# A third plain tile at the head of each FFN layer, and VectorE splitting the weight sums of four items

## What is computed

```python
def conv_ffn(h, w_up, conv_w, conv_b, w_down):
    u = causal_dwconv(h @ w_up, conv_w) + conv_b          # w_up: 1024 x 5632, 3 taps
    gate, up = jnp.split(u, 2, axis=-1)                   # 2816 columns each
    return (jax.nn.silu(gate) * up) @ w_down              # w_down: 2816 x 1024

x = x + conv_ffn(rmsnorm(x, ffn_norm[layer]), ffn_w_up[layer], ffn_conv_w[layer], ffn_conv_b[layer], ffn_w_down[layer])
```

## Time and profile before

| | us |
|---|---|
| median of 3 runs | 2227.12 (2222.16 to 2233.1) |
| profiled execution | 2223.45 |
| its span, first to last instruction | 2221.7 |
| PE / DVE / ACT / POOL busy | 2072.0 / 1409.0 / 1102.0 / 1140.4 |
| matmuls of the items (line 1184) | 4704 in the trace, 380 to 383 ns each by their spans |

### The profile page before, as it was taken

The page is one execution under the profiler, slowest core; times in us unless marked ns, Lnnn a source line. Parts: engine busy times, 40 slices in busy tenths (PEclk is TensorE's granted clock), DMA queues, the critical chain, the costliest instruction groups (busy, mean ns, idle before and its releaser), DMA issues. The chain is left out here.

```text
span 2221.7 us, 30110 instructions
## 1 busy us (share of the span) xinstructions
PE 2072.0 (93%) x11310; PEld 1002.4 (45%) x11310; DVE 1409.0 (63%) x2247; ACT 1102.0 (50%) x1653; POOL 1140.4 (51%) x856
## 2 busy tenths in 40 slices
PE   6989967889799999999999999899989999998998
PEld 3544425654344444444444444455434444443444
DVE  8788888857776575574544032795867467466452
ACT  6459856634564564554323211643566456454420
POOL 6104424216776766757584032303776766766642
PEclk8999989999999999999999999899999999999999
DMA  4001100002021211111232011101111211211112
GB/s 171 20 10 48 34 27 1 13 19 73 29 60 55 67 57 57 58 48 57 68 110 58 0 30 33 44 2 53 53 38 48 68 57 54 69 57 48 58 36 97
DMA packets 186494, 110.20 MB, mean 50 GB/s; under 512 B 4351, under 2 KB 180902, under 8 KB 186358
## 3 DMA queue, kind: packets, MB, share of 16 engines
q1 hardware_dynamic: 185894, 107.00, 16.2%
q0 software_dynamic: 464, 1.39, 0.2%
HBM read 104.18 MB, written 4.19 MB: 49 GB/s over the span
## 5 line engine op out<-in xcount | busy, mean ns | idle before, releaser
L1184 PE MATMUL ps<-arena 128*128 128x512 f16 x2784 | 612.9, 380 | 21.6 <-DVE arena L2695 9.1
L1184 PEld LDWEIGHTS ps<-arena 128*128 128x128 f16 x2784 | 272.5, 98 | 356.0 <-issue 23.6
L1184 PE MATMUL ps<-h_hi,arena 128*128 128x512 f16 x1280 | 393.8, 383 | 15.1 <-POOL arena L839 9.3
L759 POOL TENSOR_SCALAR w_scaled<-stage 128x1024 f32<-128x1024 f32 (+4 forms) x82 | 79.4, 969 | 609.2 <-PE ps L1054 419.4
L1184 PE MATMUL ps<-h_lo,arena 128*128 128x512 f16 x640 | 245.1, 383 | 0.0
L2678 DVE SCALAR_TENSOR_TENSOR work<-ps,fvec,work 128x1023 f32<-128x1023 f32 (+1 forms) x176 | 221.4, 1279 | 17.9 <-ACT work L1893 14.8
L1184 PEld LDWEIGHTS ps<-h_hi,arena 128*128 128x128 f16 x1280 | 126.1, 99 | 171.0 <-issue 14.9
L1054 PE MATMUL ps<-h_hi,arena 128*128 128x512 f16 x704 | 183.0, 381 | 2.8 <-ACT small L1799 1.7
L1054 PE MATMUL ps<-arena 128*128 128x512 f16 x708 | 158.6, 386 | 13.5 <-DVE xT L2558 6.4
L813 POOL TENSOR_TENSOR w_scaled<-stage 128x512 f32<-128x512 f32 (+2 forms) x64 | 73.4, 1148 | 175.2 <-ACT stage L1632 174.9
L1632 ACT ACTIVATE stage<-stage 128x2048 f32<-128x2048 f32 (+2 forms) x62 | 104.6, 1687 | 110.4 <-DMA stage<-in_ffn_w_up_dram 93.3
(11 more groups left out here) (358 smaller groups left out, 3779.8 us busy)
## 6 DMA issues: line engine op xcount, KB each, us to landing
stage<-in_ffn_w_up_dram SPq DMA_DIRECT2D x84, 512.0 KB, 3.8
stage<-in_ffn_w_down_dram SPq DMA_DIRECT2D x48, 384.0 KB, 3.5
stage<-in_od_w_in_dram SPq DMA_DIRECT2D x20, 512.0 KB, 3.8
stage<-in_ev_w_in_dram SPq DMA_DIRECT2D x12, 512.0 KB, 3.7
arena<-in_x_dram SPq DMA_DIRECT2D x8, 512.0 KB, 7.0
stage<-in_ffn_w_down_dram SPq DMA_DIRECT2D x16, 256.0 KB, 2.7
out_dram<-arena SPq DMA_DIRECT2D x8, 512.0 KB, 3.0
stage<-in_od_w_out_dram SPq DMA_DIRECT2D x12, 256.0 KB, 2.8
```

The lines of the kernel that those rows point to most:

```text
L759: nc.gpsimd.tensor_scalar(scaled, src, W_SCALE, 1.0, ALU.mult, ALU.mult).then_inc(w_parts, 1)
L1184: last = mm(ps[:, bank, :], left, b[:, k, :], start=(fresh and k == 0 and pss == 0), stop=(k == nk - 1 and pss == 2), skip_group_check=True)
```

## The change

Four things are done, in both layers.

1. Tile 2 is made by plain products too, behind tile 1. The two are now called `FIRST` and `SECOND` (items -2 and -1). `ITEMS` begins at tile 3, and the bank set of an item is `(p + 1) % 2`. Tile 2's halves lie in the stage buffer, are scaled one by one, split in a high part by ACT and a low part by POOL, 1024 elements each, and have no sums.
2. The orders of ACT, DVE, POOL and SP at the head of the layer are rewritten around that.
3. `split_sums` on DVE takes the place of `su_low_sums` on POOL for the items with `LAST_DOWN - PAIRS + 1 < p <= LAST_DOWN + 1`: down items 1, 2 and 3 of the four-tile group and the up item behind them (tile 17).
4. The split hidden tiles are laid out by tile (`gated`), no longer by block. The data are the same.

Core of the diff:

```diff
-            ITEMS += [("up", f) for f in range(2 if _g == 0 else _f0 + 1, _f0 + _nf)]
+            ITEMS += [("up", f) for f in range(3 if _g == 0 else _f0 + 1, _f0 + _nf)]
...
+        def by_vector(p):
+            return LAST_DOWN - PAIRS + 1 < p <= LAST_DOWN + 1
...
SP, ffn_stream
+                sp.wait_ge(w_split, unit0[f"up{layer}"] + 2)
+                load_raw(SECOND, 0)
+                load_raw(SECOND, 1)
                 for p in range(NI):
-                    if p == 0:
-                        sp.wait_ge(w_split, unit0[f"up{layer}"] + 2)
...
+                    sp.wait_ge(su_read_up, up_read(layer, raw_before(p)))
...
POOL, ffn_split
                 first_low(layer, 1)
+                second_low(layer, 0)
+                second_low(layer, 1)
                 su_first(layer, 0)
                 su_second(layer, 0)
-                su_low_sums(layer, 0)
                 top_low(layer, 1, 1, 1)
                 top_low(layer, 2, 3, 2)
+                su_low_sums(layer, 0)
                 su_first(layer, 1)
                 top_low(layer, 3, 4, 3)
                 su_second(layer, 1)
...
-                    su_low_sums(layer, p)
+                    if not by_vector(p):
+                        su_low_sums(layer, p)
...
PE, ffn
+                def plain(p):
+                    q, s = su_of(layer, p), bank_set(tile_of(p))
...
+                    for g in range(2):
+                        if p == FIRST:
+                            pe.wait_ge(*((su_read, X0 + q + 1) if g else (gate_low, GATE_LOW0 + layer + 1)))
+                        elif g == 0:
+                            pe.wait_ge(hid_f, FT * layer + tile_of(p - 2) + 1)
+                            pe.wait_ge(su_read, X0 + q + 1)
+                        else:
+                            set_free(p - 2)
+                            pe.wait_ge(su_read_up, up_read(layer, p))
...
+                plain(FIRST)
+                plain(SECOND)
...
ACT, ffn
-                if p == 0:
-                    act.wait_ge(unit_done, ring0[f"up{layer}"])
-                elif p == 1:
-                    act.wait_ge(unit_done, ring0[f"plain{layer}"] + 2)
+                if p < 2:
+                    act.wait_ge(unit_done, ring0[f"plain{layer}"] + 2 * p + 2)
...
-                        if f == 1:
-                            act.wait_ge(t_low, X0 + 3 * layer + 3)
+                        if f in (1, 3):
+                            act.wait_ge(t_low, X0 + 3 * layer + f)
...
-                su_hi_raw(layer, 0)
                 tap2(0, 0)
                 tap2(0, 1)
-                su_hi_sums(layer, 0)
+                second_raw_high(layer, 0)
+                second_raw_high(layer, 1)
+                silu(0)
+                highs(0)
                 top_high(3, 1)
                 top_high(3, 0)
                 top_high(3, 2)
-                silu(0)
-                highs(0)
-                su_scale(layer, 1)
+                su_scale(layer, 0)
                 tap2(1, 0)
                 tap2(1, 1)
-                act.wait_ge(unit_done, ring0[f"plain{layer}"] + 2)
+                su_hi_raw(layer, 0)
+                su_hi_sums(layer, 0)
+                silu(1)
+                highs(1)
+                su_scale(layer, 1)
+                tap2(2, 0)
+                tap2(2, 1)
+                act.wait_ge(unit_done, ring0[f"plain{layer}"] + 4)
                 top_high(4, 3)
...
DVE, ffn
+                def split_sums(p):
+                    nk = tiles_of(p)
...
+                    dve.wait_ge(su_hi, hi_count(layer, p))
+                    dve.wait_ge(su_sum, X0 + 4 * cross_of(layer, p) + 4)
+                    dve.wait_ge(su_read, X0 + su_of(layer, p) + 1)
+                    V.tensor_tensor(lo[:, S1:S3 + 1, :], sums_a, hi[:, S1:S3 + 1, :], ALU.subtract)
+                    V.tensor_tensor(lo[:, S2:S4 + 1, :], sums_b(nk), hi[:, S2:S4 + 1, :], ALU.subtract).then_inc(su_split, 1)
...
+                top_sum(0)
                 conv(0)
+                top_sum(1)
+                chain_begin(0)
+                top_sum(2)
+                top_sum(3)
+                chain_end(0)
                 dve.wait_ge(t_hi, X0 + 4 * layer + 2)
                 V.tensor_tensor(top_lo[:, 0], n12, top_hi[:, 0], ALU.subtract).then_inc(t_made, 1)
-                chain_begin(0)
                 conv(1)
-                chain_end(0)
+                chain_begin(1)
+                chain_end(1)
+                conv(2)
                 for p in range(NI):
...
                     cross(p, U2)
-                    if p and before is not None:
+                    if before is not None:
                         chain_begin(before)
                     cross(p, U3)
                     cross(p, C22)
-                    if p == 0:
-                        chain_begin(before)
                     if before is not None:
                         chain_end(before)
+                    if by_vector(p + 1):
+                        split_sums(p + 1)
                     cross(p, C21)
```

More of the change, by code:

```diff
@@ L409, in bank_set, with bank_of @@
             return f % 2
+        def bank_of(p):
+            return (p + 1) % 2
         def su_of(layer, p):
-            return layer * (NI + 1) + p + 1
+            return layer * (NI + 2) + p + 2
         def cross_of(layer, p):
@@ L419, in hi_count @@
         def hi_count(layer, p):
-            return layer * (2 * NI + 1) + 2 * (p + 1) + 1
+            return layer * (2 * NI + 3) + 2 * (p + 2) + 1
         def t_at(layer, f, op):
@@ L488, in by_tile, with up_read @@
             return ap.rearrange("p s (i c) -> p s i c", c=P)
+        def up_read(layer, p):
+            return MASK_STEPS + layer * (NI + 1) + p + 2
         def raw_before(p):
@@ L1095, in ffn, with set_free @@
                 first_two_units(1 + 2 * layer)
[L1097 to L1107, removed]
-                                          start=(k == 0 and pss == 0), stop=(k == KT - 1 and pss == 2))
-                    last.then_inc(unit_done, 1)
+                def set_free(p):
+                    f = tile_of(p)
+                    if f is None:
+                        pe.wait_ge(x_added, 2 + DOWN_AT[layer, ITEMS[p][1]] + 2 * ITEMS[p][2] + 2)
+                        return
+                    if not late(f):
+                        pe.wait_ge(hid_done, 2 + FT * layer + f + 1)
+                    if blocked(f) and f % 2 == 0:
+                        pe.wait_ge(kept, kept_at(layer, f, T1))
@@ L1153, in down @@
                         turns_out(8, 16)
-                def set_free(p):
-                    f = tile_of(p)
-                    if f is None:
-                        pe.wait_ge(x_added, 2 + DOWN_AT[layer, ITEMS[p][1]] + 2 * ITEMS[p][2] + 2)
-                        return
-                    if not late(f):
-                        pe.wait_ge(hid_done, 2 + FT * layer + f + 1)
-                    if blocked(f) and f % 2 == 0:
-                        pe.wait_ge(kept, kept_at(layer, f, T1))
                 def item(p):
                     j, s, nk = cross_of(layer, p), su_of(layer, p) % 2, tiles_of(p)
-                    x, z, y, v = (4 * (p % 2) + b for b in range(4))
+                    x, z, y, v = (4 * bank_of(p) + b for b in range(4))
                     if is_up(p):
@@ L1175, in item @@
                     else:
-                        right = {w: [hid_blocks(part, op, nk)[:, 0] for part in range(2)] for w, op in
+                        right = {w: [hid_blocks(part, op, nk) for part in range(2)] for w, op in
                                  ((A11, B11), (S2, T2), (S1, T1), (S3, T3), (A12, B21), (A22, T4), (S4, B22))}
@@ L1634, in scale_second @@
             def scale_second(layer, u):
-                q = su_of(layer, 0)
+                q = su_of(layer, SECOND)
                 act.wait_ge(su_landed, X0 + 32 * (q + 1))
-                last = A(raw_of(0, u), raw_of(0, u), ACT.Copy, scale=W_SCALE)
+                last = A(raw_of(SECOND, u), raw_of(SECOND, u), ACT.Copy, scale=W_SCALE)
                 if u:
@@ L1881, in tap2 @@
                     s = bank_set(f)
+                    if f < 3:
+                        act.wait_ge(unit_done, ring0[f"up{layer}"] + 2 * f + g + 1)
                     if f < 2:
-                        act.wait_ge(unit_done, ring0[(f"up{layer}", f"plain{layer}")[f]] + g + 1)
                         act.wait_ge(hid_done, 2 + c0)
                     else:
-                        j = cross_of(layer, ITEMS.index(("up", f)))
-                        act.wait_ge(cross_step, 5 * j + (C12, C21)[g])
-                        act.wait_ge(prod_done, 7 * j + (P2, P4)[g])
                         if g:
@@ L1892, in tap2 @@
                             act.wait_ge(t_sum, t_at(layer, f - 2, T4 if s else T3))
+                    if f >= 3:
+                        j = cross_of(layer, ITEMS.index(("up", f)))
+                        act.wait_ge(cross_step, 5 * j + (C12, C21)[g])
```

(1 more changed line is left out.)

99 lines of the change are left out of this document (58 added, 41 removed).

## The result

| | before | after |
|---|---|---|
| median (range; runs beside each other) | 2226.04 (2222.16 to 2233.1; 6) | 2209.14 (2208.48 to 2215.35; 6) |
| ratio of the times, 95% interval | 1 | 0.9932 (0.9917 to 0.9946) |
| profiled execution, its span | 2223.45, 2221.7 | 2215.18, 2213.1 |

What follows compares the result with a forecast made beforehand. PE, busy 93% of the span, was taken as the bound. Gains of 6.8 and 3.1 us at the layer heads and 5.2 at the group sum to 15.1, giving 2210 us; forecast range 2202 to 2216, chance 0.52.

Steps and rivals of the forecast that it cites:

- The early steps and the plain tile: Layer head: tile 0's product and chain come early, so PE runs the second plain tile, 20.7 us, without a pause.
- POOL's string ahead of tile 3: Layer head: POOL finishes item 0's weights at 592.3 us, so PE pauses about 1.5 us ahead of tile 3.
- turns: Rival: at the head DVE's work blocks POOL, 2.0 us per instruction; from 2224 us up, chance 0.07.
- The new wait inside item 0: Layer head: PE's seventh product of item 0 waits for C22 until 611.4 us, a pause of 3.6 us.
- The clock loss behind it: Layer head, behind the 3.6 us pause in item 0: a lower clock costs 1.5 us, between 0 and 2.5.
- the heads: Heads of both layers: 8.3 and 4.6 us earlier, less 1.5 each for the clock, so 6.8 and 3.1 gained.
- The splits on the path: Four-tile group: down item 1 begins 1.2 us later, items 2 and 3 cost nothing, tile 17 gains 0.6.
- The clock saved at the group: Ahead of tile 17: the pause falls from 4.54 to about 2.8 us, its clock loss from 2.5 to about 0.5.
- the group: Four splits on DVE around the four-tile group's down items: 2.6 us gained per layer, 5.2 for both.
- The heads bound by PE: Rival: no new wait in item 0, tile 4 starts 13.4 and 9.6 us earlier; 2195 us, chance 0.13.
- The weak heads: Rival: ACT late or POOL meeting DVE's token sums, each head losing 3 to 4 us more; about 2217, chance 0.20.
- the late splits: Rival: DVE gets late to the splits, which cost 1.2 us per item and gain nothing; 2215 us, chance 0.08.

Runs made afterwards that it cites:

- e4: The kernel after, with only the beginning of tile 2's chain on DVE moved back behind C22 of item 0: 2205.08 us, ratio 0.9898 to before.
- e1: The kernel after, with POOL making all low parts of the weight sums again, so only the heads stay changed: 2212.07 us, ratio 0.9935 to before.
- e3: The kernel after, with only tile 17's weight sums split by DVE and the three down items back on POOL: 2205.66 us, ratio 0.9907 to before.
- e2: The kernel before, with only the four splits moved from POOL to DVE: 2220.54 us, ratio 0.9978 to before.
- e6: The kernel after with the edits of e4 and e5 together: 2201.26 us, ratio 0.9884 to before.
- e9: The kernel after with the edits of e6 and e3 together, run again for its trace: 2194.3 us, ratio 0.9852 to before.
- e8: The kernel before, with only tile 0's chain on DVE moved ahead of the token low part and `conv(1)`: 2214.48 us, ratio 0.9951 to before.
- e5: The kernel after, with only the first `top_low` moved ahead of item 0's sums on POOL: 2207.24 us, ratio 0.992 to before.

## Why the prediction was right, point by point

The time was forecast within 1 us, and the mechanism held. But two terms of the clock were mis-sized and their errors cancel, so that the total came this near is partly luck.

**The early steps and the plain tile: right.** PE ran through both plain tiles without a pause, so the loads, copies and subtractions of tile 2 were covered. The first token sum was forecast at 2.3 us as an estimate; it took 2.29, and the hidden product ended at 560.7 against "about 559" (F itself was 0.9 later):

```profile
549.31 2.29 DVE L2702 TENSOR_TENSOR arena<-arena 128x2048 f32<-128x2048 f32 x1
...
559.43 1.22 DVE L2734 TENSOR_TENSOR ps<-ps,work 128x1024 f32<-128x1024 f32 x1
```

**POOL's string ahead of tile 3: right.** The forecast was 592.3, 42.9 us behind F; it ended 593.56 - 550.26 = 43.3 behind it, so the pause was 1.69 in place of 1.5. The free prices from the trace of before held, with no turns:

```profile
575.35 1.16 POOL L828 TENSOR_TENSOR arena<-stage,arena 128x512 f16<-128x512 f32 x1 [1.15 <-ACT arena L1699]
576.46 1.27 POOL L838 TENSOR_TENSOR arena<-w_scaled,stage 128x512 f32<-128x512 f32 x1
...
581.12 8.11 POOL L872 TENSOR_TENSOR arena<-arena 128x2048 f16<-128x2048 f32 x2
589.19 2.14 POOL L850 TENSOR_TENSOR arena<-w_scaled,arena 128x1024 f16<-128x1024 f32 x1
591.28 2.13 POOL L851 TENSOR_TENSOR arena<-arena 128x1024 f16<-128x1024 f32 x1
```

Two `top_low` take 8.11, that is 4.06 each, beside DVE's `conv`, `hidden` and chain.

**The new wait inside item 0: right in cause and place, 0.8 too long.** The forecast for C22 was 611.4, which is 62.0 behind F; it came at 61.8 (612.10 - 550.26). The pause was forecast at 3.6 ("3 to 4" among the signs) and was 2.84, mostly since tile 3 began 0.4 later behind F and C22 0.2 earlier. The chain that leads to it reads as forecast, POOL's 840 (the old 828), `silu`, `hidden`, C22:

```profile
604.68 1.27 POOL L840 TENSOR_TENSOR arena<-stage,arena 128x512 f32<-128x512 f32 x1
...
607.99 1.23 DVE L2734 TENSOR_TENSOR ps<-ps,work 128x1024 f32<-128x1024 f32 x1 [8.37 <-ACT ps L1936]
...
611.34 0.70 DVE L2715 TENSOR_TENSOR ps<-stat,ps 128x512 f32<-128x512 f32 x1
```

POOL began that instruction at 604.68 against "about 604.0", and e4 shows that this wait alone held PE there.

**The clock loss behind it: the first term mis-sized.** I took 1.5 us per layer, between 0 and 2.5. In the kernels whose pause here is 2.83 to 2.85 (after, e1, e3) it was 0 in five heads of six and 1.5 in one, layer 1 of after (132.61 against 131.13). The gross gain was 8.40 and, by e1, 4.67, against 8.3 and 4.6 forecast. So the heads brought 11.6 in the profiled execution of after and 13.1 in e1, for 9.9 forecast.

**The splits on the path: right.** Down item 1 began 0.90 us later (1.2 forecast), because DVE does them behind the chain at 0.68 each, and no other down item waited. The pause ahead of tile 17 was forecast at about 2.8, and under 3 among the signs; it was 3.11 and 2.97, released by DVE as forecast. Tile 17 came 0.37 and 0.69 earlier (0.6 forecast), by the wait for POOL's low part that "keeps it from being 2 us":

```profile
971.15 0.68 DVE L2805 TENSOR_TENSOR arena<-w_scaled,arena 128x512 f16<-128x512 f32 x1
971.75 0.68 DVE L2806 TENSOR_TENSOR arena<-arena 128x512 f16<-128x512 f32 x1
...
1000.49 1.23 DVE L2805 TENSOR_TENSOR arena<-w_scaled,arena 128x1024 f16<-128x1024 f32 x1 [2.97 <-POOL arena L841]
1001.63 1.22 DVE L2806 TENSOR_TENSOR arena<-arena 128x1024 f16<-128x1024 f32 x1
```

The low price, 1.22 for 1024 elements, was the right end, since POOL stands still while they run. What the prediction did not see is that the first three splits could stay with POOL: it took the 1.2 us as the price of the four and did not ask what each alone brought (e3).

**The clock saved at the group: the second term mis-sized.** The step "its clock loss falls from 2.5 to about 0.5" failed. T17 to M3 is 107.45 where the clock stayed up. Above that, the table has 1.66 and 1.64 for after, against 2.53 and 2.60 before: 0.9 saved per layer and not 2.0. Even the 0.9 is not shown to come of the shorter pause, since e1 has 1.52 and 1.53 behind pauses of 4.75 and 4.69. The row behind the pause of 2.38 was taken to price a pause of 2.8, and there is no slope of that kind between them. Over the seven kernels with a pause of 2.8 to 3.4 us ahead of tile 17 (after, e2 to e6 and e9), the loss of the 14 layers is 0 to 0.01 in five, 1.3 to 1.7 in eight and 2.9 in one, 1.1 in the mean. Over before, e1 and e8, with 4.5 to 5.4 us, it is 1.5 to 2.6, mean 2.15. So the group brought 2.9 for 5.2 forecast.

**The sum.** 11.6 + 2.9 = 14.5 in the stages, for 9.9 + 5.2 = 15.1. The total stands by the cancelling of +1.7 and -2.3, which nothing in the prediction foresaw.

**The rivals.** The heads bound by PE did not come about, as the wait for C22 stood. Once it is taken away and POOL's string is shorter (e6), the heads bring 12.5 and 8.4 us for that rival's 13.4 and 9.6, so its price was nearly right and its condition was not met; the time was 2201.26, and the 2194.3 of e9 has the edit of e3 besides. The weak heads and the late splits did not occur in the kernel after. Of the turns there was one, off PE's path: DVE's second token sum took 2.96 us beside POOL's low part of tile 2, for the 2.29 of the first:

```profile
553.13 4.23 POOL L866 TENSOR_TENSOR arena<-stage,arena 128x1024 f16<-128x1024 f32 x2 [6.08 <-ACT arena L1685]
```

```profile
556.54 2.96 DVE L2702 TENSOR_TENSOR arena<-arena 128x2048 f32<-128x2048 f32 x1
```

They are larger where DVE's token low part is put beside POOL (e8), at one or two instructions and not eight.

**Open.** Why the clock falls behind one pause of 2.9 us and not behind another of the same length and the same place (layers 0 and 1 of after, item 0) isn't settled. e5 lost 1.7 in both layers behind 2.94 and 2.93, and of six heads behind 2.83 to 2.85 one lost 1.5. Whether that is the 0.1 us, or the missing pause of 1.69 ahead of it, no run tells apart.

## What to carry to other kernels

Follow the released wait to the next one by building the new order of each queue instruction by instruction from the durations of the old trace: this gave two new waits within 0.4 us of where they came. Then ask of each part of a change what it brings alone. Here a reorder of two lines gave four fifths of the head's gain, and three of the four splits together cost time. A gain that shortens the work ahead of a pause may leave the pause as long as it was and, as in the trace of e5, be lost to the clock, so take the pause away first (e4) and shorten the work after (e6).

## What the runs showed of the hardware that was not expected

- The clock loss behind a pause near 3 us did not follow from its length in these traces. The same matmuls in the same places took 0, about 1.5, or up to 2.9 us more. Ahead of the small matmuls of the mixer a pause of 1.20 us was followed by 0.62 of the full clock over 9 us in the trace of after, 3.0 us longer for 120 matmuls, and by no such loss in the nine others (0.98 before).
- A DVE subtraction with both inputs in SBUF, float32 to float16, takes 0.68 us at 128x512 and 1.22 at 128x1024 while POOL is idle, just as the form that reads PSUM, and 2.29 at 128x2048 (the three of the kernel after). Beside a POOL operation that reads SBUF the last takes 3.77 (e8).
